# Turning the token rows at the start of a two-block kernel: diagonals on PE in place of scaled and turned rows, and another order of the first loads

## The reference, cut to what matters

```python
h = jnp.concatenate([meta, x], axis=1)          # 16 + 256 rows
hn = rmsnorm(h, ln_mix_w[l])
# rmsnorm: y = xf * lax.rsqrt(jnp.mean(xf * xf, axis=-1, keepdims=True) + RMS_EPS); y * w
proj = hn @ w_in                                # hybrid_mixer, 1024 features in
```

## Time and profile before

| what | value |
|---|---|
| median of 3 runs | 1608.9 us (1607.36 to 1610.53) |
| the profiled execution | 1608.27 us |
| its span, first to last instruction | 1606.5 us |
| mean granted PE clock | 0.958 of full speed |
| busy: PE, DVE, ACT, POOL | 86%, 67%, 46%, 19% |
| DMA | 417.70 MB, mean 260 GB/s |

### The profile page before, as it was taken

How to read it: one execution, slowest core, us unless ns; L and a number is a source line. 1 busy time by engine, 2 the same in 40 slices (tenths; PEclk the granted TensorE clock), 3 DMA queues, 4 the chain that set the end, 5 groups by cost and what they waited for, 6 DMA issues and landing times. The chain is left out here.

```text
span 1606.5 us, 18967 instructions
## 1 busy us (share of the span) xinstructions
PE 1379.1 (86%) x6549; PEld 993.4 (62%) x6549; DVE 1080.7 (67%) x2061; ACT 736.5 (46%) x1276; POOL 301.8 (19%) x260
## 2 busy tenths in 40 slices
PE   6998979999998787777777877778899999899987
PEld 5987978888988433233333333323497787888766
DVE  5767467875678787677777777665695465645554
ACT  5665777747454322222222222212454475567853
POOL 0000000000003564444444444443100000000000
PEclk9998999999999899989999999999999999899989
DMA  6452444444558999999999999999664456354442
GB/s 225 122 183 84 153 132 142 138 141 156 182 200 326 411 421 421 422 422 420 422 421 421 422 421 422 422 420 422 251 202 155 133 184 206 124 155 146 144 128 79
DMA packets 77806, 417.70 MB, mean 260 GB/s; under 512 B 8768, under 2 KB 8832, under 8 KB 44688
## 3 DMA queue, kind: packets, MB, share of 16 engines
q0 software_dynamic: 36864, 268.45, 40.3%
q1 hardware_dynamic: 40848, 148.06, 28.9%
HBM read 415.39 MB, written 1.08 MB: 259 GB/s over the span
## 5 line engine op out<-in xcount | busy, mean ns | idle before, releaser
L319 PE MATMUL ps<-AR 128*128 128x512 f32 (+6 forms) x1160 | 363.6, 465 | 106.5 <-ACT AR L1211 71.8
L222 DVE TENSOR_TENSOR wlo<-raw,whi 128x1024 fp32r<-128x1024 f32 x257 | 311.7, 1222 | 170.5 <-ACT whi L221 167.9
L319 PEld LDWEIGHTS ps<-AR 128*128 128x128 f32 (+2 forms) x1160 | 191.1, 198 | 269.5 <-issue 127.1
L221 ACT ACTIVATE whi<-raw 128x1024 fp32r<-128x1024 f32 x257 | 269.4, 1054 | 119.4 <-PE ps L260 99.3
L260 PE MATMUL ps<-XH,whi 128*128 128x256 f32 (+1 forms) x1032 | 306.6, 297 | 4.7 <-DVE XL L330 2.4
L319 PE MATMUL ps<-SLAB,AR 128*128 128x512 f32 x516 | 247.3, 633 | 66.7 <-ACT AR L1211 66.6
L260 PE MATMUL ps<-XL,whi 128*128 128x256 f32 (+1 forms) x1032 | 297.2, 288 | 0.0
L260 PE MATMUL ps<-XH,wlo 128*128 128x256 f32 (+1 forms) x1032 | 297.1, 288 | 0.0
L1176 POOL DMA_INDIRECT AR<-in_peer_uv,C x127 | 148.2, 1167 | 658.0 <-DVE C L1130 486.3
L319 PEld LDWEIGHTS ps<-SLAB,AR 128*128 128x128 f32 x516 | 101.2, 200 | 209.3 <-issue 120.3
L260 PEld LDWEIGHTS ps<-XH,whi 128*128 128x128 f32 x1032 | 201.1, 195 | 12.8 <-DVE XL L330 5.1
(11 more groups left out here) (243 smaller groups left out, 1187.8 us busy)
## 6 DMA issues: line engine op xcount, KB each, us to landing
raw<-in_stream SPq DMA_DIRECT2D x257, 512.0 KB, 4.2
AR<-scr SPq DMA_DIRECT2D x8, 512.0 KB, 5.2
SLAB<-in_peer_uv,C POOLq DMA_INDIRECT x129, 28.4
AR<-in_rows SPq DMA_DIRECT2D x4, 512.0 KB
AR<-in_peer_uv,C POOLq DMA_INDIRECT x127, 28.0
AR<-in_con SPq DMA_DIRECT2D x1, 1280.0 KB, 7.2
AR<-in_xin SPq DMA_DIRECT2D x2, 512.0 KB, 5.2
AR<-in_xin SPq DMA_DIRECT2D x1, 1024.0 KB, 8.7
```

The source lines that it names most:

```text
L221: a = A(lambda e: e.activation(h[:, :], r, ACT.Copy), loaded[i], free, chain=False)
L222: b = V(lambda e: e.tensor_tensor(l[:, :], r, h[:, :].bitcast(F32), ALU.subtract), a, loaded[i], free, chain=False)
L319: return PE(lambda e: e.matmul(out_ap, l, r, start=start, stop=stop, skip_group_check=onto), *after, signal=sig)
```

## The change

The second token tile is issued right behind the first one; the meta rows follow, with a semaphore of their own and without the memset. The square of the meta rows waits for them alone, the square of tile 1 for the second token tile. The scaling loop is gone. In its place DVE writes a 16-column diagonal for the meta rows (it waits for `c_ready`) and two of 128 columns, into a new buffer `XDG`, and PE multiplies the unscaled rows of each feature tile by them: the meta rows (16 partitions, 16 columns out), tile 0 and tile 1 (128 columns each). `split_to` follows as before, without the wait for `c_ready`. Only `do_split(0)` is left in the loop, behind feature tile 3; the split of chunk 1 is now the first of those that `next_chunk` emits ahead of chunk 0.

```diff
-        z0 = V(lambda e: e.memset(HX[:, 2, :], 0.0))
         x0_in = dma(SP, HX[:, 0, :], x_tiles[:, 0, :], s_x)
         s_x1 = sem("s_x1")
-        x1_in = dma(SP, HX[0:16, 2, :], meta, s_x1, z0)
         x1_in = dma(SP, HX[:, 1, :], x_tiles[:, 1, :], s_x1)
+        s_m = sem("s_m")
+        meta_in = dma(SP, HX[0:16, 2, :], meta, s_m)
         c_ready = dma(SP, C1[:, :], con1, s_c)
         c_ready = dma(SP, PAR[:, :], par, s_c)
...
-        a = A(lambda e: e.activation(junk[0:16, 0, :], HX[0:16, 2, :], ACT.Square, accum_out=ss[0:16, 2:3]), x1_in)
+        a = A(lambda e: e.activation(junk[0:16, 0, :], HX[0:16, 2, :], ACT.Square, accum_out=ss[0:16, 2:3]), meta_in)
         V(lambda e: e.tensor_tensor_reduce(junk[:, 1, :], HX[:, 1, :], HX[:, 1, :], 1.0, 0.0, ALU.mult, ALU.add, ss[:, 1:2]), x1_in)
-        r = rstd(ss[:, 0:3], D, 3, a)
+        rstd(ss[:, 0:3], D, 3, a)
         x_ready = {}
-        for c in range(5):
-            if c < 4:
-                f = slice(256 * c, 256 * c + 256)
-                V(lambda e, f=f: e.tensor_scalar(HX[0:16, 2, f], HX[0:16, 2, f], ss[0:16, 2:3], None, ALU.mult))
-                v = V(lambda e, f=f: e.tensor_scalar(HX[:, 0, f], HX[:, 0, f], ss[:, 0:1], None, ALU.mult))
-                a = A(lambda e, f=f: e.activation(HX[:, 1, f], HX[:, 1, f], ACT.Copy, scale=ss[:, 1:2]), r)
...
-                    tr(ps[b][:, 0:128], HX[:, 2, f], False, ready[0], c_ready, bank_free[b])
-                    tr(ps[b][:, 16:144], HX[:, 0, f], False)
-                    tok = tr(ps[b][:, 144:272], HX[:, 1, f], True)
...
+        XDG = place("XDG", 5120, 272)
+        V(lambda e: e.tensor_scalar(XDG[0:16, 256:272], C1[0:16, C_ID:C_ID + 16], ss[0:16, 2:3], None, ALU.mult), c_ready)
+        v = diagonals(XDG[:, 0:256].rearrange("p (i c) -> p i c", i=2), ss)
+        for k in range(8):
+            b = 4 + k % 4
+            f = slice(k * 128, k * 128 + 128)
+            mm(ps[b][:, 0:16], HX[0:16, 2, f], XDG[0:16, 256:272], True, True, False, v, bank_free[b])
+            mm(ps[b][:, 16:144], HX[:, 0, f], XDG[:, 0:128], True, True, False)
+            tok = mm(ps[b][:, 144:272], HX[:, 1, f], XDG[:, 128:256], True, True, True)
+            x_ready[k] = bank_free[b] = split_to(lambda X, k=k: X[:, k * T:k * T + T], ps[b][:, 0:T], par_(P_LNMIX + k), tok)
+            if k == 3:
+                do_split(0)
```

More of the change, by code:

```diff
@@ L380, in build @@
         x_ready = {}
-        for c in range(5):
-            if c < 4:
-                f = slice(256 * c, 256 * c + 256)
-                V(lambda e, f=f: e.tensor_scalar(HX[0:16, 2, f], HX[0:16, 2, f], ss[0:16, 2:3], None, ALU.mult))
-                v = V(lambda e, f=f: e.tensor_scalar(HX[:, 0, f], HX[:, 0, f], ss[:, 0:1], None, ALU.mult))
-                a = A(lambda e, f=f: e.activation(HX[:, 1, f], HX[:, 1, f], ACT.Copy, scale=ss[:, 1:2]), r)
[L387 to L395, removed]
-                    tr(ps[b][:, 0:128], HX[:, 2, f], False, ready[0], c_ready, bank_free[b])
-                    tr(ps[b][:, 16:144], HX[:, 0, f], False)
-                    tok = tr(ps[b][:, 144:272], HX[:, 1, f], True)
-                    x_ready[k] = bank_free[b] = split_to(lambda X, k=k: X[:, k * T:k * T + T], ps[b][:, 0:T], par_(P_LNMIX + k),
-                                                         tok, c_ready)
```

## The result

The changed kernel takes 1612.2 us in the median of 20 runs, against 1607.97 for the kernel before in 20 runs of its own. The ratio is 1.0028, 95% interval 1.0019 to 1.0037. The profiled execution has a span of 1610.3 us, 3.8 more than before. The forecast was 1606.0.

What follows compares the result with a forecast made beforehand. PE, busy 86% of the span, was taken as the bound, delayed by its late start. Loads, diagonals, multiplications, clock and DVE's splits put chunk 1 at 22.4, not 25.31: 1608.9 - 2.9 = 1606.0 us, range 1603.4 to 1608.9.

Steps and rivals of the forecast that it cites:

- DMA order: First loads: second token tile issued 1.16 us earlier, landing at 7.2 to 7.9; root ends at 10.0 to 10.6.
- PAR becomes the gate: Before the diagonals: their wait for the constants covers PAR, landing at 10.6, so PE starts at 11.5.
- Turning by multiplication: PE's first stage: two token matmuls of 0.427 and a meta matmul of 0.225 make 1.08 us per feature tile, against 0.68.
- Clock: PE's beginning: multiplications raise the clock about 4.05 us after PE's start, at 15.5, so chunk 0 runs at 2.4 GHz.
- The factor of four: Feature tiles on PE: the skill's page calls FP32 transposes 4 times faster, making a matmul 0.90 and a tile 2.03 us.
- The prediction's own signs: Beginning: PE's first matmul about 11.5, ACT's splits 1.08 apart, chunk 1 at 22.4; wrong if followers are over 1.3 apart.
- Sum: Up to the weight stream: chunk 1 starts at 22.4 in place of 25.31, set by DVE; 2.9 us gained to the end.
- rival 2: Beginning: 24 multiplications take 10.2 us, clock low through chunk 1, PE becomes the bound; 4.3 us lost, 1613.2; chance 0.04.
- rival 3: Feature tiles on PE: 2.03 us each by the skill's page, tile 3 ends about 17.9; gain 0.7, 1608.2; chance 0.02.

Runs made afterwards that it cites:

- the meta matmuls in fours: The changed kernel with its 16-row meta matmuls of four feature tiles set together ahead of those tiles' token matmuls; 1607.34 us, ratio 0.9994 to before.
- the 128-row run: The changed kernel with the meta matmul taking all 128 partitions (112 of them zero) in place of 16, still 16 columns; 1607.41 us, ratio 0.9992 to before.
- the two other executions with this stream: The changed kernel run again (1613.87 us, ratio 1.0032), and the changed kernel with the loads in the order of before (1612.76 us, ratio 1.0030).
- wide columns: The changed kernel with meta matmuls of 128 rows and 128 moving columns in place of 16 and 16; 1605.98 us, ratio 0.9982 to before.
- the new order with turns: The kernel before with only the new order of the first loads, scaling and turning as before; 1607.81 us, ratio 0.9995.
- the pure delay: The kernel before with two 128 x 1024 memsets added on DVE between the sums of squares and the root; 1609.45 us, ratio 1.0004.
- warm-up: The changed kernel with seven float32 multiplications of zeros on PE ahead of everything; 1605.43 us, ratio 0.9978 to before.
- all parts: The changed kernel with 128-row meta matmuls, seven multiplications of zeros first, diagonals waiting for C1 alone, chunk 0's split earlier; 1604.57 us, ratio 0.9977 to before.

## Why the prediction was wrong, point by point

**DMA order: right, with sizes off.** SP's second issue, landing and root moved as forecast, the root even to 9.56. PAR landed at 2.58 + 6.9 = 9.5, not 10.6, so the diagonals waited for root and PAR about alike, and PE started at 10.6 in place of my 11.5: 0.9 better than the sum. That PAR becomes the gate came true in five of the other kernels with diagonals: the first diagonal waited 0.27 to 1.07 us for it, the longest with the meta matmuls in fours.

```profile
9.85 0.22 DVE L382 TENSOR_SCALAR AR<-C,SM 16x16 f32<-16x16 f32 x1 [1.07 <-DMA PAR<-in_par]
```

**Turning by multiplication: the term that failed.** I took 0.225 for the meta matmul, with 0 and 0.45 as its ends. Measured, it added 1.69 - 0.85 = 0.84 per tile, beyond the upper end. Half of it, 0.43, is two full records whatever the columns (the 128-row run); the other half, 0.41, is the change between 16 and 128 rows, shown by the same run; in the groups of four, with two such changes in place of eight, the tiles between them are back at 0.85. So the bound of two records of a turn was a guess by form, not a bound. The trace of before had rows for the change, which the prediction doesn't use. At 2.4 GHz, in the stream:

```profile
113.47 0.29 PE L260 MATMUL ps<-XL,whi 128*128 128x272 f32 x1
113.60 0.29 PE L260 MATMUL ps<-XH,wlo 128*128 128x272 f32 x1
113.82 1.13 PE L319 MATMUL ps<-AR 16*128 16x256 f32 x4
114.87 0.39 PE L260 MATMUL ps<-XH,whi 128*128 128x272 f32 x1
115.10 0.29 PE L260 MATMUL ps<-XL,whi 128*128 128x272 f32 x1
```

The steps at the edges, 0.22 and 0.23, are 0.1 longer than the 0.13 between other 272-column records, and narrower windows show the 16-row records starting at 113.82, 114.14 and 114.35: a first step of 0.32 where the next is 0.21, and two steps of 0.52 together up to 114.87, 0.1 more twice. That is 0.4 us for one pair of changes, with other forms beside it than here, and eight of them would have put some 3.2 us into the sum. The two token matmuls cost what the earlier trace rows says. The factor of four (the Trainium skill, "TensorE: Matmul & The Clock Gate", Terms) against my 1.9 isn't borne out here: the two token matmuls of a tile take 0.85, where it would make them 1.8.

**Clock: the second step that failed.** I moved the rise of the earlier trace rows, 3.9 us after continuous 128-column multiplications, to work that has short ones in it. It came 14.4 us after PE's start, and 16.3 and 16.2 in the two other executions with this stream. With all rows but short columns it came after 11.0, with wide columns after 4.4, with the short ones set apart some 3 us after the long ones began. Right ahead of every one of these rises PE ran records of 128 rows and 128 or 272 columns one right behind the other, and with short ones among them it did not rise before chunk 0. The profile's busy times, which show PE busy throughout, don't tell one case from the other.

The prediction's own signs had it: it called itself wrong if the followers were over 1.3 apart, and they are 1.69.

**Sum.** From the changed kernel's chunk 1 at 27.46, equal rows give 2.8 back (24.66, with a PE start 0.33 later), wide columns another 2.0 (22.62), where the sum said 22.4. Small slips of the sums change nothing: chunk 1's subtract ends at 22.42 by its own terms, not 22.35, the multiplications of rival 2 take 10.4, not 10.2, and tile 3 of rival 3 ends at 17.6, not 17.9. Against the new order with turns (23.14) the multiplications without their two faults win 0.5. In the changed kernel they lose 4.3 on that, and the order's 2.2 doesn't pay for it: 25.31 - 2.2 + 4.3 = 27.4.

**Rival 2 was the case**, in its place and its kind: the 24 multiplications with a low clock made PE the bound. Its price for them, 10.2 us, was short of 13.56, and its second half (chunk 1 slow as well) didn't happen: the clock was low for only four of chunk 0's 24 matmuls and part of a fifth, and for 13 and 12 in the two other executions. So it is luck that its time, 4.3 us above before, comes out so close to the measured 4.2. I gave it 0.04 because no row showed PE busy for 14 us at the low clock. That no such row was there was no evidence: the stage at 1372 us that the earlier trace rows show has no short matmuls between the long ones.

**From the beginning to the end.** In the profiles compared the shift of the scan was the same within 0.1 at the weight splits up to 125 us. After that, low stretches of the clock fall differently from one execution to the next. Busy times by stretch, before and then the new order alone:

```profile
295.00:300.00 5.00, 4.75 (x25) 3.92 (x23) 4.69 (x7) 0.92 (x2) 0.00 (x0) 0.73 0.33 97
300.00:305.00 5.00, 3.53 (x24) 3.05 (x25) 3.97 (x7) 3.15 (x6) 0.00 (x0) 1.00 0.74 270
```

```profile
295.00:300.00 5.00, 1.79 (x5) 0.71 (x4) 3.94 (x8) 1.38 (x2) 0.00 (x0) 0.86 0.73 253
300.00:305.00 5.00, 5.00 (x21) 4.22 (x20) 4.64 (x6) 2.57 (x6) 0.00 (x0) 0.50 0.54 170
```

In that execution a longer low stretch follows, and by 328 us, at the subtract of the same weight chunk, that kernel's lead of 2.2 had become a lag of 0.6. Over the table the ratio at the end (times 1608) follows the shift at the scan, from 0.9 below it to 2.4 above; the landing in the profile of before, 0.7 later than in the other runs with the old order, accounts for 0.7 of an offset that all share, and some 1.6 either way is left. The changed kernel, 4.5 and 5.1 by its ratios for shifts of 2.15 and 2.75, is at the upper end. These are single executions, and none shows by itself what the medians owe. Whether the rest is such scatter or belongs to the change stays open; the pure delay shows only that a delay alone doesn't do it.

## What to carry to other kernels

A small matmul on PE is not cheap because it is small: here one of 16 columns cost as much as a full one of 128 (0.43 us at 1.2 GHz), and one of 16 rows between ones of 128 rows another 0.4 us. Give it the shape of its neighbours, or set such matmuls together, and where PE comes out of a long idle time, fill the columns or put idle multiplications of zeros ahead of the first real work. Price a new form only by a row of that form between the same neighbours, and look for one in the whole trace; where there is none, let the range say so.

## What was not expected of the hardware

- 16 columns and 128 columns moved cost the same 1.28 us per tile at the low clock, but the clock rose 11.0 us after PE's start with the one and 4.4 with the other.
- Changing between 16-row and 128-row float32 matmuls costs 0.41 us per pair of changes at 1.2 GHz; at 2.4 GHz a tile with it took 0.96 (warm-up) and one with 128 rows throughout 0.67 (all parts, its first two followers).
- The same 24 multiplications ran 13.2 us at 1.2 GHz without a rise in the changed kernel, and 7.5 us at 2.4 GHz without a fall in the warm-up run.
- The landing of one 512 KB load, issued at the same time, ended between 7.6 and 8.6 us in the four profiles with the old order of loads.
